# The third down unit of a gated FFN's end is split ahead of the last step's activations

## The reference, cut to what matters

```
def swiglu(x, w_gate, w_up, w_down):
    return (jax.nn.silu(x @ w_gate) * (x @ w_up)) @ w_down

x = layer_norm(alpha * x + 0.5 * swiglu(x, ffn_w_gate[l, i], ffn_w_up[l, i], ffn_w_down[l, i]),
               ln_g[l, k], ln_b[l, k])
```

## Time and profile before

| | |
|---|---|
| median of 3 runs | 1730.29 us (1729.47 to 1733.63) |
| the profiled execution, its own time | 1729.72 us |
| its span in the trace | 1727.9 us |
| PE busy | 1644.8 us (95%) |
| DVE busy | 1007.3 us (58%) |
| ACT busy | 702.1 us (41%) |
| mean granted TensorE clock | 0.958 |

### The profile page before, as it was taken

How to read it: one execution, slowest core, us unless ns; L and a number is a source line. 1 busy time by engine, 2 the same in 40 slices (tenths; PEclk the granted TensorE clock), 3 DMA queues, 4 the chain that set the end, 5 groups by cost and what they waited for, 6 DMA issues and landing times.

```text
span 1727.9 us, 24255 instructions
## 1 busy us (share of the span) xinstructions
PE 1644.8 (95%) x10565; PEld 1489.2 (86%) x10565; DVE 1007.3 (58%) x1323; ACT 702.1 (41%) x784; POOL 20.4 (1%) x78
## 2 busy tenths in 40 slices
PE   7999999998799999999999999999999988799997
PEld 6779998787699998999897999989998886599996
DVE  6576556746755557544676645475545765664446
ACT  4435444434444443443354434434433444234431
POOL 1000000000000000000000000000000000000000
PEclk9899999997899999999999999999999988699999
DMA  8326554652075555555462755555554642065651
GB/s 268 99 93 225 188 181 168 219 174 95 1 244 195 188 180 195 194 179 187 152 214 74 234 181 195 178 178 187 189 190 133 199 146 98 0 212 178 194 180 41
DMA packets 195337, 286.20 MB, mean 166 GB/s; under 512 B 9239, under 2 KB 162911, under 8 KB 195231
## 3 DMA queue, kind: packets, MB, share of 16 engines
q1 hardware_dynamic: 191823, 272.20, 47.9%
q0 software_dynamic: 3264, 11.93, 2.2%
q10 hardware_dynamic: 144, 0.52, 0.1%
HBM read 283.58 MB, written 1.05 MB: 165 GB/s over the span
## 4 chain that ended last, share of the span: by engine, by line
PE 84%; DVE 10%; ACT 4%; issue 2%; DMA 1%; ACTq 0%; SPq 0%; DVEq 0%
PE ps L371 77%; DVE wlo L282 2%; PE ps L404 2%; ACT whi L277 2%; DVE x L484 1%; DVE res L481 1%; PE ps L1623 1%; PE ps L933 1%; PE ps L931 1%; DVE xt L443 1%; PE ps L1355 1%; DMA raw<-in_mla_w_dq 1%; DVE small L762 1%; PE ps L1347 1%; DVE arena L675 0%
## 5 line engine op out<-in xcount | busy, mean ns | idle before, releaser
L371 PE MATMUL ps<-xt,whi 128*128 128x256 f32 x4016 | 728.4, 284 | 0.0
L282 DVE TENSOR_TENSOR wlo<-raw,whi 128x2048 fp32r<-128x2048 f32 (+2 forms) x263 | 583.1, 2247 | 161.7 <-ACT whi L277 161.5
L371 PEld LDWEIGHTS ps<-xt,whi 128*128 128x128 f32 x4016 | 631.7, 192 | 4.4
L371 PE MATMUL ps<-xt,wlo 128*128 128x256 f32 x2008 | 569.3, 284 | 0.0
L371 PE MATMUL ps<-whi,yt 128*128 128x512 f32 (+1 forms) x1536 | 487.1, 390 | 17.1 <-DVE wlo L282 16.1
L277 ACT ACTIVATE whi<-raw 128x2048 fp32r<-128x2048 f32 (+2 forms) x263 | 483.0, 1871 | 26.7 <-DMA raw<-in_w_out 8.6
L371 PEld LDWEIGHTS ps<-xt,wlo 128*128 128x128 f32 x2008 | 386.2, 192 | 0.0
L371 PEld LDWEIGHTS ps<-whi,yt 128*128 128x128 f32 x1536 | 289.6, 190 | 80.2 <-DVE wlo L282 21.1
L371 PE MATMUL ps<-wlo,yt 128*128 128x512 f32 (+1 forms) x768 | 298.5, 389 | 0.0
L675 DVE SCALAR_TENSOR_TENSOR arena<-arena,ps 128x512 f32<-128x512 f32 x76 | 52.2, 686 | 384.7 <-issue 299.2
L371 PE MATMUL ps<-whi,xt 128*128 128x256 f32 (+4 forms) x892 | 215.2, 329 | 5.1 <-DVE wlo L282 4.2
(11 more groups left out here) (219 smaller groups left out, 771.6 us busy)
## 6 DMA issues: line engine op xcount, KB each, us to landing
raw<-in_ffn_w_up SPq DMA_DIRECT2D x76, 1024.0 KB, 5.3
raw<-in_ffn_w_down SPq DMA_DIRECT2D x76, 1024.0 KB, 4.9
raw<-in_ffn_w_gate SPq DMA_DIRECT2D x44, 1024.0 KB, 5.3
raw<-in_diff_w_qkv SPq DMA_DIRECT2D x12, 1024.0 KB, 5.0
raw<-in_w_in_conv SPq DMA_DIRECT2D x10, 1024.0 KB, 5.2
raw<-in_w_out SPq DMA_DIRECT2D x8, 1024.0 KB, 4.9
raw<-in_w_in_mlstm SPq DMA_DIRECT2D x7, 1024.0 KB, 7.1
raw<-in_w_in_mlstm SPq DMA_DIRECT2D x8, 768.0 KB, 4.3
```

Source lines behind the costliest of these rows:

```text
L282: nc.vector.tensor_tensor(wlo[:, u.slot, 0:u.size], raw[:, u.slot, 0:u.size], whi[:, u.slot, 0:u.size].bitcast(F32), ALU.subtract).then_in ...
L371: m = nc.tensor.matmul(out_, p, q, start=first and n == 0, stop=last and n == 2, skip_group_check=True)
```

## The change

In a gated FFN's last step ScalarE splits D10 right behind silu, ahead of the wait for `f_h` and the rounding L659. VectorE splits D10 at the end of step 9, ahead of step 10's multiplication and its rest. Nothing else is moved, added or removed: the same instructions run, and the units keep their order, slots and loads. With the diff, ScalarE reaches index i+3 in place of i+2 behind silu of step 10, and VectorE reaches i+3 in place of i+2 at the end of step 9; the next call on each engine begins at X0.

```
@@ ffn_scalar
                 nc.scalar.activation(f_view(0), ps[:, f_bank(f, kind, s), :],
                                      ACT.Silu if f.gated else ACT.Relu).then_inc(f_act, 1)
-                split.to(f.unit["U", s].index + 2)
+                split.to(f.unit["U", s].index + (TAIL if f.gated and s == f.steps - 1 else 2))
                 act.wait_ge(f_h, base + s + 1)
@@ ffn_vector
                 nc.vector.tensor_tensor(h_part(s, 1), f_view(1), h_part(s, 0).bitcast(F32),
                                         ALU.subtract).then_inc(f_lo, 1)
-                split.to(min(f.unit["U", s].index + 4, f.tail[0].index + 3))
+                split.to(min(f.unit["U", s].index + (2 + TAIL if f.gated and s == f.steps - 2 else 4),
+                             f.tail[0].index + 3))
             tail_vector(dve, link, n + 1, split, f.tail[-1], f.tail[0].index + 4)
```

## The result

The changed kernel took 1708.84 us in the median of 4 executions (1700.16 to 1716.75), the kernel before 1730.03 us; the ratio is 0.990 with a 95% interval of 0.9865 to 0.9936. It is faster, but by more than was forecast, and the median lies outside the range of 1713 to 1721. The four executions are not spread around their median: they took 1701.16, 1716.52, 1700.16 and 1716.75 us. The profiled one took 1701.16 us, with a span of 1699.3 us against 1727.9. So 28.6 us have to be accounted for, where the sum made 13.75.

What follows compares the result with a forecast made beforehand. TensorE matmuls were taken to bound the kernel (busy 95%), with D10's late split stalling four gated FFN tails. Gains of 3.97 + 2.40 + 4.34 + 3.04 = 13.75 us made 1716.5, forecast as 1716.3 us, range 1713 to 1721.

Steps and rivals of the forecast that it cites:

- Where D10 waits, and the two parts that move it: Each gated FFN's tail: D10's split alone is late, 3.04 us in the first; both halves fit in idle time, costing nothing.
- What is late next: Behind D10, VectorE sets the second residual, shrinking the second tail's gain from 3.04 to 2.40 us; TensorE sets the third.
- The sum of the tails: Gains of the four gated FFN tails: 3.97 + 2.40 + 4.34 + 3.04 = 13.75 us.
- Part 4, the clock: First and third tails: clock falls behind TensorE's idle cost 1.58 and 1.31 us, both counted as given back.
- The sum: Whole kernel: the tails' 13.75 us carried unchanged through the next stages, taking the median to 1716.5, forecast 1716.3 us.
- signs of being wrong: L675 late behind the split, TensorE waiting for `f_lo` or before the transposes, or half-clock matmuls in stretches that ran full.
- The base of the sum: Whole kernel before: profiled execution 1729.72 us, median 0.57 us above it, from which the gain was subtracted.
- The clock gives nothing: Rival for the tails: the stall goes but no clock time is gained; gain 10.9 us, 1719.4 us; chance 0.20.
- The other three: Rivals: VectorE takes more back, chance 0.06; another D10 input as late, 0.05; slower, VectorE parked by D10's load, 0.02.
- The second rival: First three tails: VectorE takes more back, each keeping 1.2 to 2 us; 5.2 to 8 us whole, near 1723.5; chance 0.06.

Runs made afterwards that it cites:

- the early X0: The changed kernel with ScalarE also splitting X0 behind the last silu; 12 executions from 1700.06 to 1715.10 us, mean 1708.4.
- the lower-group look at the kernel before: Profile of the kernel before with the change in the last gated FFN alone; executions at 1716.74 to 1717.73 and 1725.94 to 1728.79 us.
- the pause that gives the gain back: The changed kernel with VectorE work before step 10's low part in each gated FFN, making D10 late again; ratio to the kernel before 1.0003.
- the late pause: The changed kernel with 1.99 us of VectorE work added ahead of the mLSTM stage; four executions from 1706.55 to 1707.39 us.
- the early pause: The kernel before with 2.4 us of VectorE work added ahead of the first stage's first norm; ratio 1.0004.

## Why the prediction was wrong, step by step

**Where D10 waits, and the two parts that move it: right.** There is no idle in front of D10, D10's low half ends 1.1 us before the multiplication, `f_lo` doesn't hold TensorE up, and no part costs anything. ScalarE's half alone shows the forecast 1.1 us of it.

**What is late next: right.** VectorE sets the second residual in the first two tails, which the early X0 proves by taking 0.55 us of the forecast 0.64 out; in the third TensorE sets it.

**The sum of the tails: right, and 0.8 us short.** The four tails gave 4.22, 2.65, 4.50 and 3.19 us against 3.97, 2.40, 4.34 and 3.04. I named some 0.2 us of waiting in front of the last residual and left it out of the tails' terms. In the first two tails that is the difference: from the second residual to the last it is now 8.83 us (838.17 to 847.00), where the second tail before had 9.08. The 0.15 us of the other two were not followed up.

**Part 4, the clock: right inside the tails.** The stretch from 832 to 836 ran at a granted clock of 1.00, and the falls of 1.58 and 1.31 us went. All profiles of this study together say it more firmly. 23 tails had TensorE's idle of 2.9 to 3.0 us, and in 14 of them the granted clock was below 1.00 at some place before the last residual; in the 25 tails without the idle, and in the four of ScalarE's half alone with its idle of 1.7 us, it never was. *TensorE: Matmul & The Clock Gate* of the Trainium skill (Part 1, "What's actually happening"), that the monitor runs freely and the place of a change differs from run to run, agrees with the third tail of the kernel before: 27.52 us in two profiles, 29.10 in one.

**The step that failed** is in "The sum": "I see nothing in the next stages that keeps an absolute time, so the gain is carried." The granted clock did not stay with the instructions: the same code met the low level at 65 us of one execution and not of another. The trace of before had stretches at the low level in both attentions, the convolution stage and the mLSTM stage, and I priced the clock's changes only in the four tails. Part 4 even says that falls "may come elsewhere"; that sentence had no term in the sum and no share in the range. One of the prediction's own signs of being wrong came true, half clock in stretches that ran full: in two of three profiles of the changed kernel the convolution stage ran at a mean granted clock of 0.95, where every profile of the kernel before has 0.97. The runs show its size. Equal code took 116.7 to 127.3 us for stage 1, 97.6 to 100.5 for the convolution stage, and 173.6 to 177.9 for the mLSTM stage. The lengths go with the granted clock of the stage. The convolution stage took 97.6 and 97.7 us at 0.98, 99.1 at 0.97 (seven profiles), and 100.1 to 100.5 at 0.95 (four). The mLSTM stage took 173.6 us at 0.84, 174.1 to 176.3 at 0.83 (seven), and 177.9 at 0.82 (four).

The base of the sum failed with it: "The profiled execution took 1729.72 us (span 1727.9), which makes 1716.0; the median is 0.57 us above it" takes the kernel before to have one time. It has two groups, and 33 of its 93 executions were near 1721.5.

Two things have to be kept apart here.

*The draw at the start.* Stage 1 is done before anything is changed. Over all runs the kernel before was in its lower group in 33 of 93 executions. The median of the first runs, 1730.29, was that of three executions which all fell in the upper one, and the changed kernel's 1708.84 is the middle between two low and two high ones; no execution of it took that time to within 7 us in that first set. The forecast of 1716.3 meets the upper group of the changed kernel (1716.25 to 1718.72), but in part by luck: in the one profile from that group (1718.72 us) the tails gave their 14.6 us, while stage 1 took 2.57 us and the convolution stage 1.08 us more than in the kernel before's first profile.

*The shift by the change.* Between the lowest groups of the two kernels the distance is larger: 1721 - 1700.6 = 20 us. Against the lower-group look at the kernel before, with the last tail as before (25.3 us), the changed kernel's first profile gains 4.21, 2.67, 6.04 and 3.2 us in the tails (the third tail had a clock fall of its own), 1.39 in the convolution stage and 2.73 in the mLSTM stage: 20.2, less 0.5 in the first two mixer stages. The shift doesn't always help, though. The changed kernel's profile of 1707.38 us had the same short stage 1 (116.79), but 1.07 us more in the convolution stage and 1.57 more in the mLSTM stage than that look, so that it gained 13.4 us and not 19.7. In all seven profiles in which D10 was as late as before, or half as late, the convolution stage took 99.1 us; with the change it took 97.7, 100.2 and 100.1. That these stages hang on when D10 comes, and not on the early splits as such, was shown by the pause that gives the gain back; that it is the clock follows from the granted clock beside the lengths. Over 93 and 18 executions the means are 1727.5 and 1708.4, 19.1 us apart, with a standard error of about 1.8. The tails explain 14.6 to 16.1, so a mean gain beyond them is likely, but it is only 1.7 to 2.6 of these errors and not shown.

**The rivals.** "The clock gives nothing" fell in its first form (the tails gave the clock's part) and missed that the clock could give more. The other three did not occur: the tails kept their forecast gain, no input of D10 was late, and all 18 executions of the changed kernel, at most 1718.72, are below all 93 of the kernel before, at least 1720.20. The second rival's sum was wrong as it stood: 1.2 to 2 us from each of three tails and the fourth's 3.04 make 6.6 to 9.0 us, not 5.2 to 8; nothing else used it.

**What stays open.** Which moment of the start puts an execution in which group, and whether the shares (33 of 93 low, and 7, 5 and 6 of 18) are the same for both kernels: for the kernel before they differed between chips, with 7 of 13 low in one set and 7 of 23 in another, and all five executions of the changed kernel between 1707 and 1711 us are from one set of eight. Whether the stages outside answer to the time that went or to TensorE's idle that went with it is open too; the late pause moved the mLSTM stage with all tails as they were, but it added 1.4 us of idle itself, and it is one profile. The single execution of 1823.8 us of the early pause is not explained.

## What to carry to other kernels

A split, copy or conversion whose input has long landed belongs in the idle time of its engine before the step that it would otherwise queue behind; look for the idle on both engines of the chain, and compare it with the duration. When a few us are taken out of a kernel whose trace has stretches at the low clock elsewhere, don't carry the sum through those stages as a constant: list the stretches at the low clock first, and put their swing into the range. Compare cut profiles, stage by stage, and list the executions; three executions don't show the groups.

## What the hardware showed that I had not expected

- One program on one core has groups of execution times 9 us apart (1720 to 1723 and 1729 to 1735 us), with nothing in between in 93 executions. The mean granted clock tells them apart: 0.964 to 0.969 and 0.955 to 0.961.
- The largest part is a stretch of small matmuls in the first attention, which ran from 65 us on at a granted clock of 0.50 in one execution (15 matmuls in 5 us) and of 1.00 in another (26), with the same code before it. In both, TensorE is counted as busy for all 5 us.
- Added work of 1.99 us made the stage behind it 6.7 us longer than in the profile that it otherwise followed, and four pauses that gave a gain of some 15 us back brought the convolution and the mLSTM stage back within 0.1 us to lengths that the kernel before has (99.1 and 176.3 us; it also has 177.9).
- An idle of 2.9 us of TensorE was followed by the low level in two of four tails of one profile, and cost 1.3 and 1.6 us there beside itself. Over all profiles it was 14 of 23 tails with an idle of 2.9 to 3.0 us, none of four with 1.7 us, and none of 25 without.
